# Index scores woven into weight units, compressed jobs with four heads side by side, and three more weight units split early

## The reference

```
x = first_block(x, p, ...)        # attention, gated MLP with a causal convolution, gated embedding
x = second_block(x, ..., depth 2) # 16 meta tokens in front, then two hybrid layers

# first block, attention: 8 heads in 2 groups of 4, three kinds, and 8 sliding-window heads
k_cmp, v_cmp = compress(kc), compress(vc)       # 31 compressed keys and values per group
p_c = softmax(q k_cmp - slope * dist) * valid   # 'cmp'
o = g0 * (p_c v_cmp) + g1 * (selected) + g2 * (window)   # 'slc', 'win'; and 'swa' apart

# second block, one layer
q, k, v, gate_a, u_b, gate_b, q_idx, k_idx, w_idx, merge = rms_norm(h) @ w_in
score = sum_h relu(q_idx[h] k_idx) * w_idx[h]   # 8 index heads
sel   = top 128 of the visible keys by score
y_a   = (attention over sel, 8 heads) * silu(gate_a) @ w_a
y_b   = (pooled u_b) * silu(gate_b) @ w_b
h     = h + (sigmoid(m_a) * y_a + sigmoid(m_b) * y_b) @ w_out
```

## Time and profile before

| | us |
|---|---|
| median of 3 runs | 1560.16 |
| lowest, highest | 1555.54, 1560.35 |
| profiled execution | 1556.19 |
| its span, first to last instruction | 1554.3 |
| PE, DVE, POOL, ACT busy | 1499.2, 952.0, 971.3, 550.9 |

### The profile page before, as it was taken

How to read it: one execution, slowest core, us unless ns; L and a number is a source line. 1 busy time by engine, 2 the same in 40 slices (tenths; PEclk the granted TensorE clock), 3 DMA queues, 4 the chain that set the end, 5 groups by cost and what they waited for, 6 DMA issues and landing times.

```text
span 1554.3 us, 24339 instructions
## 1 busy us (share of the span) xinstructions
PE 1499.2 (96%) x8516; PEld 1208.8 (78%) x8516; DVE 952.0 (61%) x2033; ACT 550.9 (35%) x1280; POOL 971.3 (62%) x1496
## 2 busy tenths in 40 slices
PE   7999999999999999999999999999998999999999
PEld 7776547678778778877989888889996877777777
DVE  6874781567676640046777788944448789894251
ACT  4446682333333310044564333341125523333100
POOL 6533415656565688776886644546888774455685
PEclk9999999999999999999999999999999999999999
DMA  7210001222222332332222211112222221121223
GB/s 257 66 48 28 28 1 46 77 71 93 93 94 94 94 104 88 96 98 77 89 69 82 69 55 55 55 55 76 95 82 70 87 88 49 48 68 55 68 95 108
DMA packets 37774, 119.42 MB, mean 77 GB/s; under 512 B 5424, under 2 KB 7600, under 8 KB 37424
## 3 DMA queue, kind: packets, MB, share of 16 engines
q1 hardware_dynamic: 36544, 116.06, 23.3%
q10 hardware_dynamic: 1136, 2.09, 0.4%
HBM read 116.02 MB, written 2.10 MB: 76 GB/s over the span
## 4 chain that ended last, share of the span: by engine, by line
PE 79%; DVE 11%; ACT 3%; POOL 3%; issue 3%; DMA 1%; SPq 0%; POOLq 0%; ACTq 0%; DVEq 0%
PE ps L778 62%; PE ps L1240 3%; PE ps L797 2%; PE ps L791 2%; PE ps L980 2%; PE ps L902 2%; POOL wlo L645 2%; PE ps L1315 1%; DVE score L2385 1%; POOL whi L641 1%; DVE score L2384 1%; PE ps L1310 1%; ACT pts L1539 1%; DVE probs L2403 1%; PE ps L1290 1%
## 5 line engine op out<-in xcount | busy, mean ns | idle before, releaser
L778 PE MATMUL ps<-hh,whi 128*128 128x512 f32 (+1 forms) x1448 | 511.4, 353 | 5.3 <-DVE hl L2177 1.7
L778 PE MATMUL ps<-hl,whi 128*128 128x512 f32 (+1 forms) x1448 | 502.8, 347 | 0.0
L778 PE MATMUL ps<-hh,wlo 128*128 128x512 f32 (+1 forms) x1448 | 501.5, 346 | 0.0
L641 POOL TENSOR_SCALAR whi<-raw 128x256 fp32r<-128x256 f32 x564 | 257.8, 485 | 332.9 <-PE ps L778 331.4
L645 POOL TENSOR_TENSOR wlo<-raw,whi 128x256 fp32r<-128x256 f32 x564 | 442.7, 816 | 11.8
L778 PEld LDWEIGHTS ps<-hh,whi 128*128 128x128 f32 x1448 | 273.9, 189 | 59.4 <-issue 11.3
L778 PEld LDWEIGHTS ps<-hh,wlo 128*128 128x128 f32 x1448 | 274.1, 189 | 34.9
L778 PEld LDWEIGHTS ps<-hl,whi 128*128 128x128 f32 x1448 | 274.0, 189 | 33.0 <-issue 0.7
L735 POOL TENSOR_TENSOR wlo<-raw,whi 128x256 fp32r<-128x256 f32 x160 | 134.7, 873 | 92.8 <-ACT whi L1586 92.8
L1959 DVE TENSOR_TENSOR tmp<-tmp 128x512 f32<-128x512 f32 x12 | 10.8, 900 | 118.3 <-ACT tmp L1624 90.0
L778 PE MATMUL ps<-plain_high,whi 128*128 128x264 f32 (+2 forms) x232 | 74.0, 319 | 6.6 <-POOL wlo L645 6.2
(11 more groups left out here) (363 smaller groups left out, 2709.9 us busy)
## 6 DMA issues: line engine op xcount, KB each, us to landing
raw<-in_w SPq DMA_DIRECT2D x197, 512.0 KB, 3.5
raw<-in_w SPq DMA_DIRECT2D x8, 256.0 KB, 3.4
x<-in_x SPq DMA_DIRECT2D x4, 512.0 KB, 8.1
out<-x SPq DMA_DIRECT2D x8, 256.0 KB, 4.4
raw<-in_w SPq DMA_DIRECT2D x12, 128.0 KB, 2.9
raw<-in_w SPq DMA_DIRECT2D x4, 384.0 KB, 3.4
cw_k<-in_cw1k SPq DMA_DIRECT2D x1, 1024.0 KB, 5.5
cw_v<-in_cw1v SPq DMA_DIRECT2D x1, 1024.0 KB, 7.4
```

What stands on the lines that cost most here:

```text
L641: ins = pool.tensor_scalar(whi[s][:, c:c + PIECE], raw[s][:, c:c + PIECE], 1.0, 0.0, ALU.mult, ALU.add)
L778: mm = pe.matmul(out, lhs, rhs, start=start and n == 0, stop=stop and n == 2)
```

## The change

1. **Head.** Loads come in quarters (128 KB, `PIECE` = 2 tiles of 8) for the first half of each of the three weight units; `wg`, `vec` and the first four tiles of x, the first two each by itself, are issued from ACT's queue ahead of its work. The splits of ACT, DVE and POOL follow in pieces of 2, 2 and 4 tiles. `spread_root` moves from the start of the eighth tile to the third token tile of the seventh.
2. **Early units.** Units 4, 7 and 8 of a layer (c = 1, 4, 5 of `qunit`) join unit 3 as extra units, in the space of `bh`/`bl` and, for the last, in that of unit 3. POOL's splits go in an order and with waits of their own, so that `whi`/`wlo` are taken for units 5, 6, 9 and 10 as soon as they are free.
3. **Woven scores.** The last unit of a slot that has index scores is held back, and one `index` step goes ahead of each quarter of its matmuls, so that the unit is interrupted three times. ACT and DVE keep their work, ACT does the `relu` copies after the slot's other units and ahead of the woven one. One `mg` unit moves to the slot before it in each layer.
4. **Compressed jobs.** The four heads' probabilities lie side by side, 32 columns each with the last cleared, and one transpose turns them into one block of 128 rows. `vcmp` (in the space of the compression weights) holds the values four times in a block-diagonal of 128 rows by 256 columns per group, the rest zero; two matmuls of 128 columns weigh them.

```diff
-        QUERY_EXTRA = [U_LAYER + l * L_UNITS + 2 for l in range(LAYERS)]
+        QUERY_EXTRA = {U_LAYER + l * L_UNITS + 2 + c: spot for l in range(LAYERS)
+                       for c, spot in ((0, 0), (1, 1), (4, 2), (5, 0))}
...
+                spot = QUERY_EXTRA[n]
+                if spot:
+                    col = (spot - 1) * D + k * P
+                    return (bl if low else bh)[:].rearrange("p k t -> p (k t)")[:, col:col + count * P]
...
+        vcmp = cw1["v"][:].rearrange("p c m -> p (c m)")[:, 0:GROUPS * REP * HD].rearrange("p (g m) -> p g m", g=GROUPS)
...
+                return home[:, 0, 0:P].rearrange("p (r k) -> p r k", r=REP)
...
-                units = ["mg0 mg1", "gb0", "ub0 mg2", "mg3", "gb1 mg4", "ub1", "mg5", "gb2 mg6", "ub2", "mg7", "gb3 mg8",
+                units = ["mg0 mg1", "gb0", "ub0 mg2", "mg3", "gb1 mg4", "ub1", "mg5", "gb2 mg6", "ub2", "mg7 mg8", "gb3",
...
-                units = ["gb0", "ub0", "mg4", "gb1", "ub1", "mg5", "mg6 gb2", "ub2", "mg7", "mg8 gb3", "ub3", "mg9",
+                units = ["gb0", "ub0", "mg4", "gb1", "ub1", "mg5 mg6", "gb2", "ub2", "mg7", "mg8 gb3", "ub3", "mg9",
...
-            sp.dma_start(raw[0][:, 0:HALF], io["w"][FIRST[0]][:, 0:HALF]).then_inc(*tick("half_in0", 0, 16))
-            sp.dma_start(wg[:], io["wg"]).then_inc(*tick("wg_in", 0, 16))
...
+            sp.dma_start(raw[0][:, 0:PIECE], io["w"][FIRST[0]][:, 0:PIECE]).then_inc(*tick("quarter_in0", 0, 16))
...
-            for half in range(2):
-                first_half(half)
-                third_half(half)
+            for k0, count in ((0, PIECE), (PIECE, PIECE), (HALF, HALF)):
+                first_piece(k0, count)
+                third_piece(k0, count)
...
                 split_extra(n)
-                split(n // 2, 1, False)
-                with pool.Fori(n // 2 + 1, (n + L_UNITS) // 2 - 1) as i:
+                pool.wait_ge(ty.sem("unit_used"), unit_ready(first))
+                split_extra(n + 1)
+                for s in range(2):
+                    split(n // 2 + 1, s, False, unit_ready(first + s))
+                split_extra(n + 4)
+                pool.wait_ge(ty.sem("unit_used"), unit_ready(n))
+                split_extra(n + 5)
+                for s in range(2):
+                    split(n // 2 + 3, s, False, unit_ready(n + 2 + s))
+                with pool.Fori(n // 2 + 4, (first + L_UNITS) // 2) as i:
...
-                    if (k, t) == (7, 0):
+                    if (k, t) == (6, 2):
                         spread_root("pre")
...
-                    for g in range(GROUPS):
-                        mm = pe.matmul(out[0:NCMP, g * HD:(g + 1) * HD], hid["v"][:, 3, g * NCMP:(g + 1) * NCMP],
-                                       cw2["v"][:, 0:HD], start=True, stop=True)
+                    for h in range(REP):
+                        for g in range(GROUPS):
+                            mm = pe.matmul(out[32 * h:32 * h + NCMP, g * HD:(g + 1) * HD],
+                                           hid["v"][:, 3, g * NCMP:(g + 1) * NCMP], cw2["v"][:, 0:HD], start=True, stop=True)
...
+                if kind == "cmp":
+                    pe.transpose(bank[:, 0:P], probs1(n).rearrange("p r k -> p (r k)"), ident).then_inc(*tick("turned", turn))
+                    return
...
+                    for c in range(2):
+                        mm = pe.matmul(X[:, 1, c * P:(c + 1) * P], vcmp[:, g, c * P:(c + 1) * P], pts[:, turn % 2, 0:P],
+                                       start=c == 0, stop=False)
...
+                    if between:
+                        index(*between[0])
...
+                    stops = {i * len(spans) * DC // len(between): between[i] for i in range(1, len(between))}
...
+                            if tok * DC + k in stops:
+                                index(*stops[tok * DC + k])
...
+                    indices = [what for kind, what in plan["side"][s] if kind == "index"]
+                    woven = spacers.pop() if indices else None
...
-                    for kind, what in plan["side"][s]:
-                        if kind == "index":
-                            index(*what)
                     for f in spacers:
                         fill(f)
+                    if woven:
+                        fill(woven, indices)
...
+            act.dma_start(wg[:], io["wg"]).then_inc(*tick("wg_in", 0, 16))
+            act.dma_start(vec[:], io["vec"]).then_inc(*tick("vec_in", 0, 16))
+            for k in range(2):
+                act.dma_start(x[:, k, META:T], io["x"][:, k, :]).then_inc(*tick(f"x_one{k}", 0, 16))
+            act.dma_start(x[:, 2:4, META:T], io["x"][:, 2:4, :]).then_inc(*tick("x_in1", 0, 16))
...
+                    for h in range(REP):
+                        rows = slice(32 * h, 32 * h + NCMP)
+                        ins = act.copy(vcmp[rows, :, h * HD:(h + 1) * HD],
+                                       G[rows, 0, 0:2 * HD].rearrange("p (g n) -> p g n", g=2))
...
+                    if n == "v":
+                        dve.memset(vcmp, 0.0).then_inc(*tick("vcmp_clear", 0))
...
+                if kind == "cmp":
+                    dve.memset(probs1(n)[:, :, NCMP:32], 0.0)
```

More of the change, by code:

```diff
@@ L585, in _ @@
             sp.dma_start(raw_third[:, HALF:DC], io["w"][FIRST[2]][:, HALF:DC]).then_inc(*tick("third_in", 2, 16))
-            for c in range(1, 4):
+            for c in range(2, 4):
                 x_pair(c)
@@ L631, in _ @@
         def _(pool):
-            elsewhere = 1
+            elsewhere = 0
             def split(i, s, first, free=None):
@@ L758, in _ @@
             elsewhere += DC
-            for l, n in enumerate(QUERY_EXTRA):
+            for l in range(LAYERS):
+                first = U_LAYER + l * L_UNITS
+                n = first + 2
                 for s in range(2):
-                    split(n // 2 - 1, s, False)
+                    split(first // 2, s, False)
                 if l:
@@ L1130, in weights_of, with lunit @@
                     return whi[n % 2], wlo[n % 2]
-                def lunit(m, out, free=(None, None), half=None):
+                def lunit(m, out, free=(None, None), half=None, between=()):
+                    if between:
+                        index(*between[0])
                     high, low = weights_of(m)
-                    for tok, (lo, n) in enumerate(cols2(l) if half is None or half[1] != "ub" else [(0, TH), (TH, TH)]):
+                    spans = cols2(l) if half is None or half[1] != "ub" else [(0, TH), (TH, TH)]
+                    stops = {i * len(spans) * DC // len(between): between[i] for i in range(1, len(between))}
+                    for tok, (lo, n) in enumerate(spans):
                         if free[tok]:
@@ L1229, in fill @@
                         else:
-                            lunit(unit_of(kind, c), G[:, mine[0]:mine[-1] + 1], [g_free[b] for b in mine], (l, kind, c))
+                            lunit(unit_of(kind, c), G[:, mine[0]:mine[-1] + 1], [g_free[b] for b in mine], (l, kind, c), between)
                         for tok, b in enumerate(mine):
@@ L1893, in _ @@
                         exped2(s + 2)
-                    for kind, what in plan["side"][s]:
-                        if kind == "index":
-                            index(*what)
                     for f in spacers:
                         fill(f)
+                    for what in indices:
+                        index(*what)
+                    if woven:
+                        fill(woven)
                 a_high(plan["slots"] - 2)
@@ L1986, in _, with second_low @@
                 .then_inc(*tick("head_low", ("gate", 1)))
-            def second_low(half):
-                ks = slice(half * HALF, half * HALF + HALF)
-                dve.wait_ge(*at("head_high", ("value", 1, half)))
+            def second_low(k0, count):
+                ks = slice(k0, k0 + count)
+                dve.wait_ge(*at("head_high", ("value", 1, k0)))
                 dve.tensor_tensor(wvl[:, ks, P:2 * P], raw[1][:, ks], wvh[:, ks, P:2 * P].bitcast(F32), ALU.subtract)\
-                    .then_inc(*tick("head_low", ("value", 1, half)))
-            second_low(0)
+                    .then_inc(*tick("head_low", ("value", 1, k0)))
+            second_low(0, PIECE)
             dve.wait_ge(*at("vec_in", 0))
```

93 lines of the change are left out of this document (51 added, 42 removed).

## The result

The changed kernel takes 1568.8 us (median of 5 runs, 1566.7 to 1570.4), beside 1556.9 for the kernel before in the same comparison: a ratio of 1.0062, with a 95% interval of 1.0044 to 1.0081. It is 0.6% slower, some 10 to 12 us. I had forecast 1542, with a range of 1529 to 1553. The profiled execution has a span of 1567.7 us, against 1554.3.

A forecast was written before the change was run, and what follows sets the result against it. TensorE, busy 1499 of 1554 us, was taken as the bound. Head -2.5, compressed jobs -3.7, early units 0, clock +2 and woven scores -12.5 sum to -16.7, giving 1539.5; the median was put at 1542, range 1529 to 1553.

The forecast's parts named there:

- Head, -2.5: At the kernel's start: values begin 3.1 us earlier through reordered loads, for a gain of 1.8 to 3.1 us, 2.5 taken.
- what does not shift is GpSimd: In the head: GpSimd's second split of the next stage still ends by 30.77, so 1.8 us is the lower gain.
- Early units, 0: At second-block layer starts: weight waits go, but VectorE's chain sets the same end, so nothing is gained; other bound 8.7 us.
- The clock, +2: At both layer starts: one longer stop lowers TensorE's clock, costing 1 us per layer, bounds 0 to 4.4 us.
- a rival: Layer starts and slots: lower clock 2.4 us, dear drain up to 6 worse; gain 8 to 14; within a shared 0.21.
- Woven scores, -12.5: In five slots of the second block: interleaving index scores with unit matmuls gains 12.5 us, bounds 4 and 17.
- the term of 3.7 that is given back to VectorE: In the slots: VectorE, near 92% full in the first layer, makes TensorE wait for `weighted` rows, losing 3.7 us.
- 10.7 + 5.5: In the slots: 10.7 us from removed waits after deductions, plus 5.5 us from two low-clock stretches going away.
- The first rival: In the slots: VectorE becomes the bound, leaving a gain of 5 to 12, about 1551; chance 0.21, shared with the pages' rules.
- The drain: At 15 woven interruptions: tiling-mode changes drain TensorE; about 0.1 us each counted, 0.4 more each would be 6 us worse.
- Compressed jobs, -3.7: Eight attention jobs: one turn replaces four, saving 0.68 us each, about half in the second group; 3.7 us, bounds 2 and 5.5.
- The slower rival: In the slots: each woven pair stalls the unit because ScalarE reaches `relu` late, making the kernel slower; chance 0.05.

The follow-up runs named there:

- the runs of one part at a time: Four kernels, each the kernel before with one part of the change: head 1.0041, early units 1.0055, woven scores 0.9986, compressed jobs 1.0002.
- Even mended: The kernel before with the head change only, the second weight's last half split ahead of x's third and fourth tiles, squares one pair later: ratio 1.0005.
- the filled stop: The kernel before with the early units only, plus 36 unneeded matmuls per layer in TensorE's stop before the rotated queries: ratio 0.9997.
- part 3: The kernel before with only the woven index scores added: ratio 0.9986.
- the best kernel: The kernel before with woven scores and units reordered so that more work follows the last woven unit: 1545.2 us, ratio 0.9912.

## Why the prediction was wrong

By the runs of one part at a time, the forecast missed by 10.3 us at the woven scores, 8.9 at the head, 6.6 at the early units and 4.0 at the compressed jobs.

**Head, -2.5: the step that failed is "what does not shift is GpSimd".** I had its split end at 30.77 and took it as the next bound, 1.8 us ahead of PE's need. But the edit moves VectorE's last piece of `raw[1]` behind two more tiles of x. The load of the next unit waits, by way of GpSimd's step behind it, for this piece, and the one behind it stands in the same queue: 2.3 us later at the piece, 2.1 at the first split, 3.8 at the end of the second. A moved step has to be followed into the load that its buffer releases. Even mended, the head gains 0.8 us in its trace and nothing that the runs can tell, so GpSimd left less room than my lower bound of 1.8.

**Early units, 0: right. The clock, +2: mis-sized, measured 6.4 in the trace and 8.6 in the runs.** VectorE's chain ends the stop as predicted, 4.8 and 4.9 us long, and no gain comes from the weights. The price of a stop I took at 1 us, by a unit with a mean clock of 0.71. The stretches here are 6.8 us at 0.50 whole, which can cost up to 3.4 us each. By the rule of the Trainium skill, "TensorE: Matmul & The Clock Gate", section on HAM oscillation, that idle gaps bring the lower clock back, both layers pay: the traces agree (stops of 4.80 and 4.91 us, then 6.8 us at 0.50), and the filled stop shows that the idle time of PE brings it. I gave this rule 2.4 us and left it within a rival; with my upper bound of 4.4 even that was low.

**Woven scores, -12.5: the gross gain was right, the term of 3.7 that is given back to VectorE failed.** The trace of part 3 gains 13.1 us before the two last stops, 1.1 behind the first, and 2.8 more without the stop of 2.83: 17.0 in all; I had 16.2 (10.7 + 5.5). What is given back is 13.8: 2.8 + 5.4 + 5.6. I had read VectorE's mean share of 120 us and called it 92% full. The mean hides the order: VectorE waits for the last score and then has some 32 us of selection in a row, at 94%. I also wrote that its idle time inside the clusters is only moved. It is moved, but behind the last score, where TensorE has less work left to hide the selection. The first rival names VectorE, but leaves a gain of 5 to 12; the clock that fell behind each stop made it dearer than that. That this is the cause is shown from both sides. With the unit taken earlier on both sides of slot 9, the stop of the first layer stays (4.01 us); with one more unit between the last score and the stop, the stop and the low clock go, and the kernel goes from -2.2 to -13.7 us.

**The drain.** Scores of 64 rows inside matmuls of 128 rows cost little: pairs start 2.74 us apart, 1.10 for the pair and 1.64 for the quarter of a unit, against 1.50 undisturbed. That is 0.14 us per interruption; I had 0.1. By the rule of the Trainium skill, "TensorEngine Tiling (Array Packing)", section Tiling Modes, a change of mode drains TensorE; at the 0.4 us more that I had allowed for it the pairs would be 3.1 apart. The trace shows no such gap.

**Compressed jobs, -3.7: right for the first four (2.3 against my 2.7), wrong for the second four.** I had called VectorE 96% full there and still counted half a gain. It was none: the longer wait met the clock, which the sum has at nothing for this part. Over the runs the lower clock can have taken up to 4 us (an estimate from the means of 0.989 and 0.992), the whole forecast; why it falls more with these jobs stays open.

**The slower rival** (each woven pair stalls on `relu`) is refuted: no `relu` wait is left. The kernel became slower in a way that I had priced as small: long stops in five places (one in the head, two ahead of `qi`, two in the slots), and the lower clock behind each.

## What to carry to other kernels

Taking waits away ahead of a busy engine doesn't remove them, it gathers them; several waits under 2 us cost their own time, one of 4 to 5 us costs the clock as well. If the stop can't go, give TensorE something to do in it. When a producer's work is spread out to help one engine, count what work is left between its *last* item and the deadline of whoever consumes it, and move independent work there: here this one edit turned -2 us into -14.

## What the runs showed of the hardware

- Each stop of PE of 3.95 us or more behind the first value matmul was followed, within the stop or right behind it, by 3.4 to 6.8 us at 1.2 GHz: in the changed kernel at 29.6, 794.3, 1002.9, 1212.4 and 1380.6 us. Stops of 2.83 and 2.56 us were too, at 936.0 and 189.0; those of 2.82 or 2.83 in four other traces were not, the best kernel's among them.
- With the same instructions the clock falls in the first block's attention in some executions and not in others (17 us at 1.2 GHz against 3.4). What decides it stays open: the traces show no difference ahead of it but a shift of PE against the kernel before. At 96 us it lies between 1.0 us early and 2.6 late in the kernels without the compressed jobs, and it does not tell the clock in any simple way (3.4 us at 1.2 GHz at a shift of -1.0, 17.1 at -0.7, none at 0.0).
- With the compressed jobs the clock fell for longer there: 20.5 to 23.9 us in four profiles, beside at most 17.1 in nine without. The mean clock of the runs says the same in both comparisons: 0.989 beside 0.992, and 0.993 beside 0.998.
